# Modulation weights in eighths through a ring of four, six tiles of them on TensorE

## The chip, the cores and the metric

One core of one Trainium2 chip runs the whole program. The metric is the device time of one execution in microseconds (us). Engines are named as in the profile: PE is TensorE (matmuls), PEld its weight loads, DVE VectorE, ACT ScalarE, SP SyncE, which issues the DMAs. PEclk is the granted TensorE clock; 1.00 is 2.4 GHz and half of it is 1.2 GHz.

## The reference

One layer of a transformer is run for 128 context tokens and 512 latent tokens with the same weights: a feed-forward network (FFN0), a token mixer (an mLSTM and an attention branch), and a second feed-forward network. Each of the three is shifted, scaled and gated by a modulation vector that is a product of the conditioning vector with one large matrix, `w_mod`:

```python
def trunk_layer(x, mod, n_pre, n_post, f_in, f_out, mix_w, ctx):
    sh0, sc0, g0, sh1, sc1, g1, sh2, sc2, g2 = jnp.split(mod, N_MOD, axis=-1)
    h = rms_norm(x, n_pre[0]) * (1 + sc0) + sh0
    x = x + 0.5 * g0 * rms_norm(swiglu(h, f_in[0], f_out[0]), n_post[0])
    h = rms_norm(x, n_pre[1]) * (1 + sc1) + sh1
    y, st = token_mixer(h, *mix_w, ctx)
    x = x + g1 * rms_norm(y, n_post[1])
    ...
# reference():
        mod_ctx = (jax.nn.silu(c_ctx) @ w_mod[l] + b_mod[l])[None, None, :]
        mod_lat = (jax.nn.silu(c) @ w_mod[l] + b_mod[l])[:, None, :]
```

Here D_MODEL is 1024, D_FF 2816, N_MOD 9: `w_mod` has 1024 rows and 9216 columns, and only two vectors, one of each group of tokens, are multiplied with it.

## The kernel before

Matrices are streamed from HBM in tiles of 512 KB (128 partitions x 1024 numbers) through four `raw` buffers. Every fp32 weight is split into a high and a low part: ACT casts the high part (`whi`, L1441), DVE subtracts it for the low one (`wlo`, L1979), and PE makes three products (high-high, low-high, high-low). SP issues the loads in program order from one queue; the semaphores on which it waits are those by which a buffer comes free. All orders are written out by hand, engine by engine.

FFN0 runs in three phases p=0, 1, 2 over its 2816 inner columns. A phase has input products (in p=0 as eight-wide loops at L819 to L821, in p=1 and p=2 partly as pairs of seven products i=0..6 at L789 to L791) and then output work: in p=0 and p=1 eight out tiles v=0..7 (`out_tile`, L926 to L928), in p=2 the *border*. An out tile with v other than 3 and 7 has two halves o=0, 1 of 15 matmuls each. The splits of tile v+2 are made on ACT and DVE while PE works at tile v; the cast must wait until PE has left the tile whose buffer it takes. The border adds up FFN0's last out tiles by rows of 128 tokens (`row_w`, L891 to L893), updates the residual `x_tok`, normalises it (L2267 is the first step of that on DVE), and at once starts the mixer's first product with `first_w` (L1012 to L1014).

The first columns of `w_mod` are done at the start; 14 later tiles of 512 columns (n=0..13), each with eight blocks of 128 rows (k=0..7), are worked off inside FFN0 beside the products. Two ways are in use:

- *Multiplied:* DVE multiplies every block by the vectors' numbers and adds it into `macc` (`over_k`: `ts` at k=0, L2343, else `stt`, L2346; two of them for a block, one for each group of tokens). When all eight k are in, PE sums over the partitions with 0/1 weights `pick` (`sum_mod`, L973): four matmuls, one for each quarter of the 128 columns of the array. The trace records each of these fp32 matmuls twice.
- *Direct:* PE multiplies the block as it was loaded with the vectors as weights (`silc_win`) (`direct_mod`, L987). The block's k decides the quarter: even k goes to quarters 0 and 1, odd k to quarters 2 and 3, half of the 512 columns each.

Before, a transfer (`load_mod`, L524) brings two k (512 KB, a quarter of a tile), the ring `mw` has two such places, tiles 7 to 10 are direct and the other ten multiplied. A direct call has two k, so four matmuls, in all four quarters; the 16 calls stand in the pairs n=0..7 of p=1 after the products i=1 and i=4. `sum_mod` stands in out tiles v=2 and v=5 and in two of the pair loops. DVE multiplies some blocks beside the pairs of p=1.

Of the kernel before, what the change touches and what calls it, by code (L numbers as in the profile page):

```python
# [21 lines left out]
P = 128  # L22
# [30 lines left out]
MOD_PARTS, MOD_RING = 4, 2  # L53
PART_K = KC // MOD_PARTS
FIRST_K = KC - PART_K
MOD_DIRECT = (7, 8, 9, 10)
PAIR_PARTS = tuple(((n, part), (n, part + 1)) for n in MOD_DIRECT for part in (0, 2))
MOD_ORDER = ([(n, part) for n in range(MOD_DIRECT[0]) for part in range(MOD_PARTS)]
             + [one for pair in PAIR_PARTS for one in pair]
             + [(n, part) for n in range(MOD_DIRECT[-1] + 1, MOD_LATER) for part in range(MOD_PARTS)])  # L60
# [86 lines left out]
def build(nc, a):  # L147
    ctx = ExitStack()
    with ctx:
# [57 lines left out]
        mw = at("mw", [P, MOD_RING * PART_K, MOD_W], F32, mw_at)  # L207
        macc_at = mw_at + MOD_RING * PART_K * MOD_W * 4
# [26 lines left out]
        def row_home(l, u):  # L235
            one, two = blocks[l], others[l]
            if l == 0:
                return ((mw_at, mw_at + whole), (mw_at + 2 * whole, two), (one, one + whole), (one + 2 * whole, one + 3 * whole),
                        (one + 4 * whole, two + 4 * whole), (two + whole, two + 2 * whole))[u]
            if l == 2:  # L240
                at_ = (one, two)[u % 2] + u // 2 * 2 * whole
                return at_, at_ + whole
            return ((one, one + whole), (one + 2 * whole, one + 3 * whole), (one + 4 * whole, two + 4 * whole),
                    (two, two + whole), (two + 2 * whole, two + 3 * whole))[u]
# [4 lines left out]
                   for u, home in enumerate(((others[0] + 3 * whole, mw_at + 3 * whole),  # L249
                                             (mw_at + 4 * whole, cst_at + 5 * P * 4)))]  # L250
# [257 lines left out]
        def _(sp):  # L508
# [4 lines left out]
            def load_mod(n, part):  # L513
                where = MOD_ORDER.index((n, part))
                if where >= MOD_RING:
# [3 lines left out]
                    else:  # L519
                        sp.wait_ge(mod_mul, 2 * PART_K * parts_until(before, False))  # L520
                slot = where % MOD_RING
                src = a["w_mod"][n][:, part * PART_K * MOD_W:(part + 1) * PART_K * MOD_W]
                to = mw[:, slot * PART_K:(slot + 1) * PART_K, :].rearrange("p k c -> p (k c)")
                sp.dma_start(to, src).then_inc(mod_in[slot], 16)  # L524
# [38 lines left out]
            def ffn(f, base):  # L563
                j0 = 0
                for p, nj in enumerate(PHASES):
# [18 lines left out]
                    if f == 0 and p == 0:  # L584
                        load_mod(0, 0)
                        load_mod(0, 1)
                        for u in range(4, 8):
                            load_in(u)
                            if u > 5:
                                load_mod(0, u - 4)  # L590
                        for u in range(8, tiles):
                            load_in(u)
                            load_mod(u // 4 - 1, u % 4)
                        for v in range(4):
                            load_out(v)
                            load_mod(3, v)
                        for v in range(4, KC):
                            load_out(v)
                            if v < 6:
                                load_mod(4, 2 * v - 8)  # L600
                                load_mod(4, 2 * v - 7)
                            elif v == 7:
                                load_mod(5, 0)
                                load_mod(5, 1)
                    elif f == 0 and p == 1:
                        load_in(0)
                        load_mod(5, 2)
                        load_mod(5, 3)
                        load_in(1)
                        load_in(2)  # L610
                        load_mod(6, 0)
                        load_mod(6, 1)
                        load_in(3)
                        load_mod(6, 2)
                        load_mod(6, 3)
                        for n in SEVEN[1]:
                            for one in PAIR_PARTS[n]:
                                load_mod(*one)
                            load_next(2 * n + 4)
                            load_next(2 * n + 5)  # L620
                        load_mod(11, 0)
                        load_mod(11, 1)
                        load_out(4)
                        load_out(5)
                        load_mod(11, 2)
                        load_mod(11, 3)
                        load_out(6)
                        load_mod(12, 0)
                        load_out(7)
                        load_mod(12, 1)  # L630
                    elif f == 0 and p == 2:
                        for u in range(4):
                            load_in(u)
                            if u < 2:
                                load_mod(12, 2 + u)
                            elif u == 2:
                                load_mod(13, 0)
                                load_mod(13, 1)
                            else:
                                load_mod(13, 2)  # L640
                                load_mod(13, 3)
# [54 lines left out]
            load_post(0)  # L696
            load_residual(a["x_tok"], slice(2, NT))
            mix(2, RAWS)
# [63 lines left out]
        def _(pe):  # L762
            mm, tp = pe.matmul, pe.transpose

            def seven(f, p, n, base):
                g = SEVEN_FROM[f][p] + n
                gt, ut = pair_tiles(base, n)
                for i in range(7):
# [24 lines left out]
                    if f == 0 and p == 1 and i in (1, 4):  # L793
                        direct_mod(*PAIR_PARTS[n][i // 4])
                    if f == 0 and i == 2:
                        if p == 1 and n == 0:
                            sum_mod(6)
                        elif p == 2 and n == 0:
                            sum_mod(13)
# [2232 lines left out]
```

## Time and profile before

| what | us |
|---|---|
| median of 3 runs (1717.27 to 1719.05) | 1718.79 |
| the profiled execution, its own time | 1718.85 |
| its span in the trace | 1716.9 |
| PE busy | 1684.5 (98%) |
| PEld busy | 1545.1 (90%) |
| DVE busy | 1104.6 (64%) |
| ACT busy | 733.3 (43%) |
| chain that ended last: PE / DVE / ACT / DMA | 87% / 5% / 4% / 2% |

FFN0 with everything that the change touches lies in the first 532 us of the span: p=0 until some 213 us, p=1 until some 387, p=2 with the border until 532. A row of the timeline gives the start, the duration, the engine and line, the operation, and in brackets how long the engine sat idle before it and what ended that. Rows of PE overlap, since a matmul's duration contains its way through the array: the distance of two starts says what one costs. "x8" joins eight like records in a row.

### The profile page before, as it was taken

How to read it: one execution, taken by the hardware profiler on the slowest of the kernel's cores; microseconds unless marked ns; L12 is line 12 of the kernel's file. 1: busy time of each engine (PE TensorE's matmuls, PEld its weight loads, DVE VectorE, ACT ScalarE, POOL GpSimd, SP SyncE). 2: the span in 40 equal slices, each digit the busy share in tenths (PEclk: the TensorE clock that was granted, in tenths of full speed). 3: DMA queues.
4: the chain of work that ended last, by engine and by line, in shares of the span. 5: the costliest groups of instructions: out<-in, count | busy, mean ns of one | idle time of the engine just before them, and what ended most of it. 6: DMA issues, size and time to landing. Idle time of an engine off the chain costs nothing.

```text
span 1716.9 us, 27871 instructions
## 1 busy us (share of the span) xinstructions
PE 1684.5 (98%) x11255; PEld 1545.1 (90%) x11255; DVE 1104.6 (64%) x1881; ACT 733.3 (43%) x1370; POOL 0.2 (0%) x4
## 2 busy tenths in 40 slices
PE   8999999999999999999999999999999999999998
PEld 6899799879979989999999988989989988998997
DVE  5688787769855424555536877775546844882785
ACT  6332244314565322343355555553474433541453
POOL 0000000000000000000000000000000000000000
PEclk9999999999999999999999999999999999999999
DMA  9344544542424225332342311102522221322234
GB/s 376 121 147 152 163 169 147 180 140 75 139 95 148 74 74 108 91 100 80 82 155 80 114 53 42 41 23 68 208 73 76 81 92 62 96 89 86 73 96 151
DMA packets 60966, 189.65 MB, mean 110 GB/s; under 512 B 7928, under 2 KB 17064, under 8 KB 58920
## 3 DMA queue, kind: packets, MB, share of 16 engines
q1 hardware_dynamic: 60840, 187.89, 33.6%
q8 instruction: 89, 1.46, 0.3%
q14 instruction: 37, 0.30, 0.1%
HBM read 170.67 MB, written 16.54 MB: 109 GB/s over the span
## 4 chain that ended last, share of the span: by engine, by line
PE 87%; DVE 5%; ACT 4%; DMA 2%; issue 1%; DVEq 0%; ACTq 0%
PE psum L819 9%; PE psum L821 9%; PE psum L820 9%; PE psum L789 8%; PE psum L790 7%; PE psum L791 7%; PE psum L926 4%; PE psum L927 3%; PE psum L928 3%; PE psum L1347 2%; PE psum L1329 2%; PE psum L891 2%; PE psum L893 2%; PE psum L892 2%; PE psum L1307 2%
## 5 line engine op out<-in xcount | busy, mean ns | idle before, releaser
L1979 DVE TENSOR_TENSOR wlo<-raw,whi 128x1024 fp32r<-128x1024 f32 x120 | 146.9, 1224 | 278.0 <-ACT whi L1441 277.8
L1441 ACT CAST whi<-raw 128x1024 fp32r<-128x1024 f32 x120 | 125.6, 1047 | 248.9 <-PE psum L928 131.4
L819 PE MATMUL psum<-g_hi,whi 128*128 128x320 f32 x656 | 209.5, 319 | 0.2 <-ACT gate L1797 0.2
L821 PE MATMUL psum<-g_hi,wlo 128*128 128x320 f32 x656 | 202.8, 309 | 0.0
L820 PE MATMUL psum<-g_lo,whi 128*128 128x320 f32 x656 | 202.8, 309 | 0.0
L819 PEld LDWEIGHTS psum<-g_hi,whi 128*128 128x128 f32 x656 | 123.2, 188 | 4.9 <-issue 1.9
L926 PE MATMUL psum<-whi,g_hi 128*128 128x512 f32 x320 | 126.4, 395 | 0.0
L927 PE MATMUL psum<-wlo,g_hi 128*128 128x512 f32 x320 | 125.8, 393 | 0.0
L928 PE MATMUL psum<-whi,g_lo 128*128 128x512 f32 x320 | 125.4, 392 | 0.0
L820 PEld LDWEIGHTS psum<-g_lo,whi 128*128 128x128 f32 x656 | 123.3, 188 | 0.7
L821 PEld LDWEIGHTS psum<-g_hi,wlo 128*128 128x128 f32 x656 | 123.2, 188 | 0.0
L2346 DVE SCALAR_TENSOR_TENSOR macc<-mw,silc,macc 128x512 f32<-128x512 f32 x140 | 95.5, 747 | 3.5 <-DMA mw<-in_w_mod 3.1
L819 PE MATMUL psum<-h_hi,whi 128*128 128x320 f32 x272 | 84.6, 311 | 2.3 <-DVE sb L2462 2.3
L821 PE MATMUL psum<-h_hi,wlo 128*128 128x320 f32 x272 | 84.1, 309 | 0.0
L820 PE MATMUL psum<-h_lo,whi 128*128 128x320 f32 x272 | 84.1, 309 | 0.0
L926 PEld LDWEIGHTS psum<-whi,g_hi 128*128 128x128 f32 x320 | 60.7, 190 | 15.0 <-issue 2.5
L928 PEld LDWEIGHTS psum<-whi,g_lo 128*128 128x128 f32 x320 | 60.8, 190 | 12.8
L927 PEld LDWEIGHTS psum<-wlo,g_hi 128*128 128x128 f32 x320 | 60.8, 190 | 12.4
L789 PE MATMUL psum<-h_hi,whi 128*128 128x320 f32 x220 | 69.0, 314 | 2.9 <-DVE y L2497 2.5
L789 PE MATMUL psum<-t_hi,wlo 128*128 128x320 f32 x228 | 71.0, 311 | 0.0
L789 PE MATMUL psum<-t_hi,whi 128*128 128x320 f32 x228 | 70.5, 309 | 0.0
L791 PE MATMUL psum<-t_hi,whi 128*128 128x320 f32 x228 | 70.5, 309 | 0.0
(449 smaller groups left out, 4473.6 us busy)
## 6 DMA issues: line engine op xcount, KB each, us to landing
raw<-in_w_ffn_in SPq DMA_DIRECT2D x88, 512.0 KB, 3.7
raw<-in_w_mix SPq DMA_DIRECT2D x77, 512.0 KB, 4.1
mw<-in_w_mod SPq DMA_DIRECT2D x56, 512.0 KB, 4.5
raw<-in_w_ffn_out SPq DMA_DIRECT2D x44, 512.0 KB, 3.6
mw<-in_w_mod SPq DMA_DIRECT2D x8, 1024.0 KB, 16.1
gate<-gate_keep SPq DMA_DIRECT2D x24, 320.0 KB, 4.7
gate_keep<-gate SPq DMA_DIRECT2D x20, 320.0 KB, 4.7
x_keep<-x_tok SPq DMA_DIRECT2D x2, 2560.0 KB, 9.0
```

The source lines that it names most:

```text
L789: mm(out, wh[:, k, :], th[:, k, :], start=(first and k == 0), stop=False, skip_group_check=more)
L790: mm(out, wh[:, k, :], tl[:, k, :], start=False, stop=False, skip_group_check=more)
L791: last = mm(out, wl[:, k, :], th[:, k, :], start=False, stop=(k == KH - 1), skip_group_check=more)
L819: mm(out, wh[:, k, :], hi[:, k, cols], start=(k == 0), stop=False)
L820: mm(out, wh[:, k, :], lo[:, k, cols], start=False, stop=False)
L821: last = mm(out, wl[:, k, :], hi[:, k, cols], start=False, stop=(k == nk - 1))
L926: mm(out, g_hi[:, j, tok], wh[:, o, :], start=(j == 0), stop=False)
L927: mm(out, g_hi[:, j, tok], wl[:, o, :], start=False, stop=False)
L928: return mm(out, g_lo[:, j, tok], wh[:, o, :], start=False, stop=(j == KC - 1))
L1441: copy((to or whi[t.slot])[:, :, :], raw[t.raw][:, :, :]).then_inc(w_hi, 1)
L1979: tt(lo[:, :, :], raw[t.raw][:, :, :], hi[:, :, :].bitcast(F32), ALU.subtract).then_inc(raw_free, 1)
L2346: last = stt(acc, w, by, acc, ALU.mult, ALU.add)
```

## The change

The diff's core; helper lines that only follow are cut.

```diff
-MOD_PARTS, MOD_RING = 4, 2
-FIRST_K = KC - PART_K
-MOD_DIRECT = (7, 8, 9, 10)
+MOD_RING, FIRST_K = 4, 5
+MOD_DIRECT = (6, 7, 8, 9, 10, 11)
+SLOT_OUT = ([(4, 0), (4, 1), (4, 2), (7, 0)], [(4, 3), (4, 4), (4, 5), (7, 1)], [(7, 2)], [(4, 6), (4, 7), (7, 3)],
+            [(5, 0), (7, 4)], [(5, 1), (5, 2), (7, 5)], [(5, 3), (5, 4), (7, 6)], [(5, 5), (5, 6), (5, 7), (7, 7)])
+SLOT_PAIR = [[((6, 8, 9, 10)[n // 2], 4 * (n % 2) + o) for o in range(4)] for n in range(8)]
+SLOT_OUT2 = ([(12, 0), (11, 0)], [(12, 1), (12, 2), (12, 3), (11, 1)], [(12, 4), (12, 5), (12, 6), (11, 2)], [(12, 7), (11, 3)],
+             [(13, 0), (11, 4)], [(13, 1), (13, 2), (13, 3), (11, 5)], [(13, 4), (13, 5), (13, 6), (11, 6)], [(13, 7), (11, 7)])
...
             mix(L_GATE, 2)
             load_post(0)
+            mix(2, RAWS)
             load_residual(a["x_tok"], slice(2, NT))
-            mix(2, RAWS)
...
-                    if f == 0 and p == 1 and i in (1, 4):
-                        direct_mod(*PAIR_PARTS[n][i // 4])
+                    if f == 0 and p == 1 and i in (1, 2, 3, 5):
+                        direct_mod(*SLOT_PAIR[n][{1: 0, 2: 1, 3: 2, 5: 3}[i]])
+                    if f == 0 and i == 2 and n == 0:
+                        sum_mod(5 if p == 1 else 13)
...
+                        if f == 0 and o == 0:
+                            direct_mod(*(SLOT_OUT2 if p else SLOT_OUT)[v][-1])
...
-            def direct_mod(n, part):
+            def direct_mod(n, k):
...
-                for o in range(PART_K):
-                    k = part * PART_K + o
-                    for half in range(2):
-                        last = mm(mod_part(2 * (k % 2) + half, half), silc_win[:, k, skip:skip + MOD_COLS],
-                                  mw[:, slot * PART_K + o, half * MOD_HALF:(half + 1) * MOD_HALF], start=False, stop=False)
+                for half in range(2):
+                    last = mm(mod_part(2 * (k % 2) + half, half), silc_win[:, k, skip:skip + MOD_COLS],
+                              mw[:, slot, half * MOD_HALF:(half + 1) * MOD_HALF], start=False, stop=False)
...
-                            if f == 0 and v in (2, 5):
-                                mod = (4, 11)[p] + v // 5
+                            if f == 0 and v == 4:
+                                mod = (4, 12)[p]
...
+                        if f == 0:
+                            split(Tile(base + 2 * n + 5), row_weights(0, 3, base + 2 * n + 2)[0], gt.n + 3)
+                            split(Tile(base + 2 * n + 6), row_weights(0, 4, base + 2 * n + 2)[0], ut.n + 3)
...
-                for u in range((3, 5, 3)[l], ROW_TILES[l]):
+                for u in range((5, 5, 3)[l], ROW_TILES[l]):
...
+                            if f == 0 and v not in (0, 4):
+                                multiply_slot((SLOT_OUT2 if p else SLOT_OUT)[v])
+                            elif f == 0 and p == 0 and v == 0:
+                                multiply_slot(SLOT_OUT[0])
...
+                            if f == 0 and (v == 4 or p == 1 and v == 0):
+                                multiply_slot((SLOT_OUT2 if p else SLOT_OUT)[v])
```

In words:

- **Transfers.** One k a transfer (256 KB), a ring of four places; 112 transfers instead of 56. In the first stage of p=0, five instead of six k of tile 0 are taken after the normalised rows.
- **Direct tiles.** Tiles 6 to 11 are direct, 0 to 5, 12 and 13 are multiplied. A direct call has one k, so two matmuls, in two of the four quarters. There are 48 calls: one in every out tile of p=0 (tile 7) and of p=1 (tile 11), behind o=0 or, at v=3 and 7, behind the tile, and four in every pair of p=1 (behind i=1, 2, 3 and 5).
- **Multiplied blocks.** None beside the pairs of p=1; tiles 4, 5, 12 and 13 beside the out tiles, before the split in most tiles, behind it (`multiply_slot` at the loop's end) at v=4 of both phases and v=0 of p=1. `sum_mod` stands at v=4 and in the pair n=0.
- **Border.** Row weights u=3 and 4 are split in the last pair of p=2; at the border only u=5 is left, and some buffers change places. SP issues two tiles of the mixer's weights before the 1.5 MB of residual rows instead of behind them.

SP at the first out tiles of p=1, before (`raw` from `w_ffn_out` are out tiles, those from `w_ffn_in` belong to p=2; "x2" joins two like ones):

```order
L511 DMA raw_69<-in_w_ffn_out 128x1024 [waits raw_free]
L511 DMA raw_70<-in_w_ffn_out 128x1024 [waits raw_free]
L524 DMA mw<-in_w_mod 128x1024 [waits mod_mul] x2
L511 DMA raw_71<-in_w_ffn_out 128x1024 [waits raw_free]
L524 DMA mw<-in_w_mod 128x1024 [waits mod_mul]
L511 DMA raw_72<-in_w_ffn_out 128x1024 [waits raw_free]
L524 DMA mw<-in_w_mod 128x1024 [waits mod_mul]
```

And now; `mod_mul` counts DVE's multiplications, `mod_pe` direct calls:

```order
L512 DMA raw_69<-in_w_ffn_out 128x1024 [waits raw_free]
L512 DMA raw_70<-in_w_ffn_out 128x1024 [waits raw_free]
L524 DMA mw<-in_w_mod 128x512 [waits mod_mul]
L524 DMA mw<-in_w_mod 128x512 [waits mod_pe]
L512 DMA raw_71<-in_w_ffn_out 128x1024 [waits raw_free]
L524 DMA mw<-in_w_mod 128x512 [waits mod_mul] x3
L524 DMA mw<-in_w_mod 128x512 [waits mod_pe]
L512 DMA raw_72<-in_w_ffn_out 128x1024 [waits raw_free]
```

The first `mod_mul` row brings (12, 3) and waits for the product with (12, 0); (11, 1), which PE takes in out tile v=1, is the `mod_pe` row behind it.

DVE at out tiles v=0 and 1 of p=1, before (the first of a tile's products, with `pick`, stands ahead of v=0's split):

```order
L1979 TENSOR_TENSOR wlo_76<-raw_70,whi_74 128x1024 [waits w_hi]
L2026 TENSOR_TENSOR g_lo<-sb_80,g_hi 128x640 [waits g_hi_s]
L2352 COPY pick<-pick_row 128x32 [waits rows_zero,mod_done,ev0,ev1]
L2352 COPY pick<-pick_row 128x32
L2343 TENSOR_SCALAR macc<-mw,silc 128x512 [waits mod_in0]
L2343 TENSOR_SCALAR macc<-mw,silc 128x512
L2346 SCALAR_TENSOR_TENSOR macc<-mw,silc,macc 128x512 [waits mod_mul] x2
L2346 SCALAR_TENSOR_TENSOR macc<-mw,silc,macc 128x512 [waits mod_mul,mod_in1]
L2346 SCALAR_TENSOR_TENSOR macc<-mw,silc,macc 128x512 [waits mod_mul] x3
L1979 TENSOR_TENSOR wlo_75<-raw_71,whi_73 128x1024 [waits w_hi]
```

And now:

```order
L1969 TENSOR_TENSOR wlo_76<-raw_70,whi_74 128x1024 [waits w_hi]
L2016 TENSOR_TENSOR g_lo<-sb_80,g_hi 128x640 [waits g_hi_s]
L1969 TENSOR_TENSOR wlo_75<-raw_71,whi_73 128x1024 [waits w_hi,ev0,ev1]
L2342 COPY pick<-pick_row 128x32 [waits mod_done,rows_zero]
L2342 COPY pick<-pick_row 128x32
L2333 TENSOR_SCALAR macc<-mw,silc 128x512 [waits mod_in0]
L2333 TENSOR_SCALAR macc<-mw,silc 128x512
L2336 SCALAR_TENSOR_TENSOR macc<-mw,silc,macc 128x512 [waits mod_mul,mod_in2]
```

The split of tile v+2 (`wlo_75<-raw_71`) has moved ahead of the products with (12, 0).

PE in the pairs of p=1, before, around the first direct call:

```order
L791 MATMUL psum<-t_hi_1_170,wlo_75 128x320
L987 MATMUL psum<-mw,silc_win 32x256 [waits mod_in0,cols_in]
L987 MATMUL psum<-mw,silc_win 32x256 x3
L789 MATMUL psum<-h_hi,whi_74 128x320 [waits ld_x4_then_act_kept,ld_x3_then_prod_lo]
L790 MATMUL psum<-h_lo,whi_74 128x320
```

And now, around one of the 48:

```order
L779 MATMUL psum<-t_hi_1_170,whi_73 128x320
L974 MATMUL psum<-mw,silc_win 32x256 [waits mod_in0]
L974 MATMUL psum<-mw,silc_win 32x256
L777 MATMUL psum<-h_hi,wlo_75 128x320 [waits ld_x4_then_act_kept,ld_x3_then_prod_lo]
L778 MATMUL psum<-h_lo,wlo_75 128x320
```

A call has two matmuls instead of four, and there are three times as many calls.

## Rows read from the trace of the kernel before

**Rows 1.** The page, busy time of the engines.

```profile
PE 1684.5 (98%) x11255; PEld 1545.1 (90%) x11255; DVE 1104.6 (64%) x1881; ACT 733.3 (43%) x1370; POOL 0.2 (0%) x4
```

**Rows 2.** Waits of PE by line: releaser, us in total, times, longest.

```profile
PE psum L973 <- DVE macc L2346: 4.1, 2, 2.2
PE psum L789 <- DVE y L2497: 2.5, 1, 2.5
PE psum L891 <- DVE row_w L1979: 2.3, 1, 2.3
PE psum L863 <- DVE y L2267: 2.3, 1, 2.3
PE psum L819 <- DVE sb L2462: 2.3, 1, 2.3
PE psum L1012 <- DVE g_lo L2272: 1.0, 1, 1.0
```

**Rows 3.** Busy time by windows: window, length, then each engine; PEclk third last.

```profile
213.00:320.00 107.00, 107.00 (x776) 97.29 (x775) 82.60 (x138) 48.89 (x93) 0.00 (x0) 1.00 0.46 154
362.00:371.00 9.00, 6.80 (x29) 4.60 (x28) 3.88 (x5) 0.00 (x0) 0.00 (x0) 0.81 0.40 121
384.00:393.00 9.00, 6.42 (x43) 5.65 (x46) 8.86 (x15) 3.49 (x7) 0.00 (x0) 1.00 0.01 3
```

**Rows 4.** Timeline of PE around a direct call in a pair of p=1.

```profile
216.42 0.31 PE L790 MATMUL psum<-t_lo,wlo 128*128 128x320 f32 x1
216.57 0.31 PE L791 MATMUL psum<-t_hi,wlo 128*128 128x320 f32 x1
216.81 0.64 PE L987 MATMUL psum<-mw,silc_win 128*32 128x256 f32 x8
217.38 0.41 PE L789 MATMUL psum<-h_hi,whi 128*128 128x320 f32 x1
217.63 0.30 PE L790 MATMUL psum<-h_lo,whi 128*128 128x320 f32 x1
```

**Rows 5.** Timeline of PE in the mixer: matmuls in two halves of the array.

```profile
985.51 1.31 PE L1347 MATMUL psum<-sbb,av 128*64 128x128 f32 x20
986.76 1.13 PE L1307 MATMUL psum<-ak,aq 64*128 64x256 f32 x8
```

**Rows 6.** Timeline of PE, first and last matmul of half a tile (p=1, v=5).

```profile
359.50 0.39 PE L926 MATMUL psum<-whi,g_hi 128*128 128x512 f32 x1
...
362.68 0.39 PE L928 MATMUL psum<-whi,g_lo 128*128 128x512 f32 x1
```

**Rows 7.** Timeline of ACT, then DVE, in out tiles v=5 and 6 of p=1.

```profile
359.76 1.05 ACT L1441 CAST whi<-raw 128x1024 fp32r<-128x1024 f32 x1 [5.75 <-PE psum L928]
371.17 1.05 ACT L1441 CAST whi<-raw 128x1024 fp32r<-128x1024 f32 x1 [10.37 <-PE psum L928]
373.57 0.88 DVE L2343 TENSOR_SCALAR macc<-mw,silc 128x512 f32<-128x512 f32 x2
```

**Rows 8.** DMA issues: count, KB, median us to landing; then one of the chain.

```profile
cs<-in_state_C SPq DMA_DIRECT2D x2, 256.0 KB, 2.9
o_x<-x_tok SPq DMA_DIRECT2D x2, 256.0 KB, 2.0
akc<-in_cache_k SPq DMA_DIRECT2D x1, 256.0 KB, 2.8
358.54 3.90 DMA mw<-in_w_mod
```

**Rows 9.** Timeline of DVE ahead of two waits of PE (58.8 and 386.8).

```profile
55.22 2.73 DVE L2346 SCALAR_TENSOR_TENSOR macc<-mw,silc,macc 128x512 f32<-128x512 f32 x4
...
379.77 2.74 DVE L2346 SCALAR_TENSOR_TENSOR macc<-mw,silc,macc 128x512 f32<-128x512 f32 x4 [1.34 <-DMA mw<-in_w_mod]
```

**Rows 10.** Timeline at the border: ACT, then DVE.

```profile
483.44 1.05 ACT L1441 CAST first_w<-raw 128x1024 fp32r<-128x1024 f32 x1 [3.66 <-DMA raw<-in_w_mix]
...
487.35 0.75 DVE L2267 TENSOR_SCALAR y<-x_tok,roots 128x1024 f32<-128x1024 f32 x1 [0.38 <-ACT roots L1550]
```

More of the change, by code:

```diff
@@ L52 @@
 MOD_HALF = MOD_W // 2
-MOD_PARTS, MOD_RING = 4, 2
-PART_K = KC // MOD_PARTS
-FIRST_K = KC - PART_K
-MOD_DIRECT = (7, 8, 9, 10)
[L57 to L60, printed above, removed]
+MOD_RING, FIRST_K = 4, 5
[5 more added lines that the diff above has]
+             [(13, 0), (11, 4)], [(13, 1), (13, 2), (13, 3), (11, 5)], [(13, 4), (13, 5), (13, 6), (11, 6)], [(13, 7), (11, 7)])
+MOD_ORDER = ([(n, k) for n in range(4) for k in range(KC)]
+             + [one for slots in (SLOT_OUT, SLOT_PAIR, SLOT_OUT2) for slot in slots for one in slot])
 MOD_MULTIPLIED = [n for n in range(MOD_LATER) if n not in MOD_DIRECT]
@@ L237, in row_home @@
             if l == 0:
[L238 to L239 removed]
+                return ((mw_at, mw_at + whole), (mw_at + 2 * whole, two), (one, one + whole), (two + whole, cst_at + 5 * P * 4),
+                        (one + 4 * whole, two + 4 * whole), (one + 2 * whole, one + 3 * whole))[u]
             if l == 2:
@@ L511, in load, with load_mod @@
                 sp.dma_start(raw[t.raw][:, :, :].rearrange("p k c -> p (k c)"), src).then_inc(raw_in[t.raw], 16)
-            def load_mod(n, part):
-                where = MOD_ORDER.index((n, part))
+            def load_mod(n, k):
+                where = MOD_ORDER.index((n, k))
                 if where >= MOD_RING:
@@ L519, in load_mod, with load_slot @@
                     else:
-                        sp.wait_ge(mod_mul, 2 * PART_K * parts_until(before, False))
+                        sp.wait_ge(mod_mul, 2 * parts_until(before, False))
                 slot = where % MOD_RING
-                src = a["w_mod"][n][:, part * PART_K * MOD_W:(part + 1) * PART_K * MOD_W]
-                to = mw[:, slot * PART_K:(slot + 1) * PART_K, :].rearrange("p k c -> p (k c)")
-                sp.dma_start(to, src).then_inc(mod_in[slot], 16)
+                src = a["w_mod"][n][:, k * MOD_W:(k + 1) * MOD_W]
+                sp.dma_start(mw[:, slot, :], src).then_inc(mod_in[slot], 16)
+            def load_slot(slot):
+                for n, k in slot:
+                    load_mod(n, k)
             def pick(tiles, n):
@@ L594, in ffn @@
-                        for v in range(4):
+                            load_mod(u // 4 - 1, u % 4 * 2)
+                            load_mod(u // 4 - 1, u % 4 * 2 + 1)
+                        for v in range(KC):
                             load_out(v)
[L596 to L604, printed above, removed]
-                    elif f == 0 and p == 1:
[L606 to L615, printed above, removed]
-                        for n in SEVEN[1]:
[L617 to L622, printed above, removed]
@@ L2064, in seven @@
                     if p == 2:
-                        for u in range(1, 3):
+                        for u in range(1, 3 if f else 4):
                             split(Tile(base + 2 * n + 2 + u), row_weights(2 * f, u, base + 2 * n + 2))
                     pair_product(n, s)
+                    if p == 2 and f == 0:
+                        split(Tile(base + 2 * n + 6), row_weights(0, 4, base + 2 * n + 2))
                     if p < 2:
@@ L2206, in first_normed @@
                     if k >= FIRST_K:
[L2207 removed]
+                        over_k(0, k - FIRST_K)
             def add_square(l, m):
@@ L2275, in first_split @@
                     split(Tile(nxt + u), first_weights(l, u, nxt))
-                for u in range((3, 5, 3)[l], ROW_TILES[l]):
+                for u in range((5, 5, 3)[l], ROW_TILES[l]):
                     split(Tile(base + u), row_weights(l, u, base))
@@ L2352, in pick_rows, with multiply @@
                     copy(pick[:, g * MOD_COLS:(g + 1) * MOD_COLS], pick_row[:, first:first + MOD_COLS])
-            def multiply(n, part, ks=range(PART_K)):
-                if part == 0 and ks.start == 0:
+            def multiply(n, k):
+                if k == 0:
                     dve.wait_ge(rows_zero, 1)
@@ L2358, in multiply, with multiply_slot, later_k @@
                     pick_rows(n)
-                over_k(n, part, ks)
-            def later_k(part):
-                if part == MOD_PARTS - 1:
+                over_k(n, k)
+            def multiply_slot(slot):
+                for n, k in slot[:-1]:
+                    multiply(n, k)
+            def later_k(first, last):
+                if last == KC:
                     dve.wait_ge(pick_in, 2)
                     pick_rows(0)
-                over_k(0, part, range(PART_K))
+                for k in range(first, last):
+                    over_k(0, k)
             def take_rows():
```

117 lines of the change are left out of this document (50 added, 67 removed).

## The prediction

> **What bounds the kernel now.** I read the busy times first. PE is busy 1684.5 of 1716.9 us [rows 1], so the span can shrink only by PE's own work, by PE's waits, or by the start and the end. Next the windows: over the pairs of p=1 PE is busy 107.00 of 107.00 us [rows 3]. Whatever is put between two matmuls there lengthens the span one to one, and work taken from DVE (64% busy) gives nothing by itself. Then PE's waits by line [rows 2]: in the part that the change touches there are seven of 1 us and more, 14.5 us in sum (4.1 + 2.5 + 2.3 + 2.3 + 2.3 + 1.0), and these alone can be won. A wait can cost more than its length: around the wait at 365 the granted clock is 0.81 over 9 us, around that at 386.8 it is 1.00 [rows 3]. A mean of 0.81 with levels 1 and 0.5 means 9 x 0.19 / 0.5 = 3.4 us at 1.2 GHz, in which 1.7 us of work are lost. Of the six waits over 1.9 us, four (the two at L973, L891, L863) are followed by it and two (L819, L789) are not.
>
> **The change part by part.**
>
> *Direct calls, +22.0.* What one costs I take from the distance of starts: from the last matmul ahead of it (216.57) to the second behind it (217.63) are 1.06 us; two steps of the 320-wide matmuls would be 2 x 0.147 (from 216.42 to 216.57 is one), so the call costs 0.77 [rows 4]. I read its eight records (four matmuls) as two rounds of four, each quarter doing its own matmul's two records one after the other. The new call has two matmuls in two quarters: half the work, but each quarter still has two records to do. The nearest row is one in which the array is split in two: 20 records of L1347 take 985.51 to 986.76, 1.25 us, so ten rounds of two at 0.125 [rows 5]; different parts of the array run beside each other, records of one part do not. A round of 256 columns is then 0.22 to 0.25, two of them 0.43 to 0.50, and some 0.33 of the 0.77 (0.27 to 0.34) are going into and out of the split form. So the new call keeps both rounds and both transitions: 0.77, with half the array idle. Bounds: half of it (0.38), if a call costs by its matmuls, and 0.77; I take 0.77, the end that rows 5 speak for. Calls: 16 are removed and 48 added, 32 x 0.766 = +24.5. Two `sum_mod` fewer (10 become 8; eight records in the same form) give -1.5. In three places a direct call stands right behind a `sum_mod`, so one pair of transitions is shared: 3 x 0.33 = -1.0. Together +22.0; with 0.38 a call it would be 48 x 0.38 - 12.3 - 2.5 = +3.5.
>
> The Trainium skill ("TensorEngine Tiling (Array Packing)", section Tiling Modes, Key Properties) says that a change of the tiling mode drains the engine and that tiles work independently, in parallel. That speaks against cutting calls in half, and the trace agrees: some 0.3 of the 0.77 are no rounds. By that rule, too, the sum would be 1741.
>
> *DVE's multiplications, 0 by themselves.* Two tiles fewer are 32 operations of 0.75, 24 us of an engine that PE seldom waits for. One k more in the first stage falls into gaps of 1.3 us that DVE has there between the steps of the normalisation; if it did not fit, it would cost 0.9.
>
> *New waits, +10.0, and the clock behind them, +5.1.* A direct call makes PE wait for a DMA where before only DVE did. SP issues in order, and a place of the ring of four comes free by the block four earlier. At p=1, (11, 1) stands behind (12, 3), which waits for DVE's product with (12, 0); (11, 5) likewise behind (13, 3) and (13, 0); at p=0, (7, 5) takes the place of (5, 0) itself. All three products now stand behind the split of tile v+2 on DVE, and that split behind ACT's cast, which starts when PE has left the tile before. The chain from the start s of a tile, in rows of v=5 and v=6: the cast starts at s + 0.26 (359.50 to 359.76 [rows 6, 7]); from the cast (371.17) to the first product (373.57) are 2.40, and the two products take 0.88 [rows 7]. So the place is free at s + 3.55, and SP issues at s + 3.6, for (11, 1) and (11, 5) one issue (0.4) later. No row has a load of 256 KB of `w_mod`; others of 256 KB land in 2.0 to 2.9 [rows 8], a lone one of 512 KB in 3.90 [rows 8]. I take 2.8 (a load from HBM of the same size), bounds 2.0 and 3.9. The weights are there at s + 6.4 for (7, 5) and s + 6.8 for the others. PE asks for them behind o=0, 15 matmuls after s: 359.50 to 362.68 are 14 steps, so s + 3.4 [rows 6]. PE waits 3.0 + 3.5 + 3.5 = 10.0 (with 2.0 a load 7.6, with 3.9 13.3). All three lie in tiles of lines 926 to 928, where both waits of before were followed by the low clock; 3 x 1.7 = 5.1, or nothing if the clock holds as at 386.8. (7, 1) is the next closest and lands about when it is asked for; I put it at 0.
>
> The Trainium skill ("DMA: Bandwidth & Descriptors", section Anatomy of one DMA) gives 2.0 us and the bytes by 436 GB/s, an estimate of 2.6 for 256 KB. The rows with 2.8 and 2.9 agree. The three waits would each be 0.2 shorter, and the time 1740.
>
> *Old waits that go, -12.3.* The two waits of `sum_mod` for DVE (4.1 us [rows 2]) go, as tiles 4 and 12 are summed at v=4, after the blocks have long been multiplied: -1.9 - 2.2, and 1.7 of clock each, -7.5. The wait of L819 for L2462 (2.3) stands behind four multiplications, 55.22 to 57.95 [rows 9], which now come before the split: -2.3. The wait of L789 for L2497 (2.5) comes from DVE running late after a wait of 1.34 for a load and the multiplications at 379.77 [rows 9], which are gone from there: -2.5.
>
> *Border, -2.5.* Three waits stand here: L891 2.3, L863 2.3, L1012 1.0 [rows 2]. Splitting u=3 and 4 sooner moves the first one to u=5, whose raw weights land hardly sooner: about 0. The 1.5 MB of residual are issued ahead of the mixer's weights, which keep ACT idle for 3.66 until 483.44 [rows 10]; issued ahead of it they come about 4 us sooner, ACT and DVE split `first_w` sooner, and the normalisation at 487.35 [rows 10] starts some 2.5 earlier. Behind it stands the chain of ACT and DVE for each 128 tokens, which the end of the border follows (the wait at L1012 is its sign), so the 2.5 come through once. Bounds: 0, if the residual (two of its rows are now later by two issues) takes the place of the weights; 9.0, if all three waits and both clock losses go (2.3 + 2.3 + 1.0 + 2 x 1.7). I take 2.5, nearest to the idle time of ACT.
>
> *SP.* It issues 112 instead of 56 transfers at some 0.4; its queue waits for semaphores most of the time, so the 24 us are hidden, save the 0.4 counted above.
>
> Sum, from the profiled execution's 1718.85 (0.06 above the median, so they can be used alike): 1718.85 + 22.0 + 10.0 + 5.1 - 12.3 - 2.5 = **1741**.
>
> **The rivals.**
>
> *A, the loads come in time.* If DVE's split and products were ahead of PE (the cast earlier, loads at 2.0), PE would not wait: 1741 - 15 = 1726. For: DVE has 24 us less to do. Against: the order on DVE, and a cast bound to the end of PE's tile.
>
> *B, old waits stay.* The two waits of `sum_mod` might come back at v=4, if the loads of tiles 4 and 12 are held up by the same queue: 1741 + 7.5 = 1749. For: the ring holds 1 MB before and after, so SP runs no further ahead. Against: in p=0 the blocks of tile 4 are spread over v=0, 1 and 3 and DVE has slack at v=2.
>
> *C, the other side: calls cost by their matmuls.* If the records of two quarters fill one round, as four records of the same form seem to do in [rows 4], and the transitions hide behind the weight loads, a call costs near 0.2 and not 0.77: 48 x 0.2 - 12.3 - 2.5 = -5.2, and if the new waits are hidden as well, 1718.85 - 5.2 - 12.3 - 2.5 = 1699; with the new waits 1714. With the waits, it decides below a price of (14.8 of the removed calls and sums + 12.3 + 2.5 - 15.1) / 48 = 0.30 a call. Against: [rows 5], and the 0.3 outside the rounds. A call of one round (0.77 - 0.22) gives 1741 - 48 x 0.22 = 1730, still slower.
>
> *D, the whole border is won:* 1741 - 6.5 = 1734.5, still slower.
>
> **How the numbers follow.** Forecast (with D and the dearer or cheaper loads in it) 0.74, its own range 1733 to 1749; A, or a call of one round, 0.14, 1725 to 1732; B 0.07; C 0.05, of which 0.02 fall within 0.2%. 0.2% (3.4 us) is about what a measurement of this kernel can tell from no change. From 1725 to 1750 the cases of the forecast, A and B count 0.95 by their centres; their tails and C leave out under 2 in 10. Slower 0.95, same 0.02, faster 0.03.
>
> **What would show it.** The calls: 48 groups of four records at the `direct_mod` line, with 0.77 between the neighbours' normal steps; 0.55 or less fails the largest term. The waits: PE waiting for a DMA `mw` at that line three times, at v=5 of p=0 and at v=1 and 5 of p=1, 3 to 3.5 us each, with PEclk near 0.8 behind them. The old waits: no wait of `sum_mod` for `macc`, none of L819 and L789 in FFN0. The border: ACT's `first_w` some 4 us sooner after the end of p=2, and the first mixer matmul behind the border 2.5 sooner. The forecast is wrong if PE's busy time does not grow by some 20 us, or if a wait that I do not list is longer than 3 us.

## The result and the profile after

The changed kernel takes 1741.84 us (median of 4 runs, 1740.57 to 1743.75), the kernel before on the same chip 1718.92. The ratio is 1.0136, with a 95% interval of 1.0118 to 1.0153: 22.9 us slower. The forecast was 1741.0, from 1725 to 1750. The profiled execution of the changed kernel took 1743.75, with a span of 1741.8; it is 1.9 above the median, and the terms below are read from it.

The page, busy time of the engines, answering to [rows 1]:

```profile
PE 1707.4 (98%) x11303; PEld 1547.4 (89%) x11303; DVE 1084.9 (62%) x1845; ACT 733.3 (42%) x1370; POOL 0.2 (0%) x4
```

DVE has given up 19.7 us of work and PE has taken 22.9 us more. Now the waits of PE by line (releaser, us in total, times, longest), answering to [rows 2]; only those of FFN0 and the border are shown. L974 is `direct_mod`, L876 the border's row product, L848 the normalisation, L999 the mixer's first product:

```profile
PE psum L974 <- DMA mw<-in_w_mod: 12.5, 4, 4.6
...
PE psum L876 <- DVE row_w L1969: 2.0, 1, 2.0
PE psum L999 <- DVE g_lo L2264: 2.0, 2, 1.2
...
PE psum L848 <- DVE y L2259: 0.6, 1, 0.6
```

The waits of `sum_mod` for `macc` (4.1), of L789 (2.5) and of L819 (2.3) are gone, as forecast. In their place stands one line that waits for a DMA, 12.5 us in four waits. Where they are, and what the clock does behind three of them: first PE's timeline (idle time before and what ended it in brackets), then the busy times by windows, PEclk third last.

```profile
161.99 0.63 PE L974 MATMUL psum<-mw,silc_win 128*32 128x256 f32 x4 [0.53 <-DMA mw<-in_w_mod]
...
195.89 1.07 PE L974 MATMUL psum<-mw,silc_win 128*32 128x256 f32 x4 [3.02 <-DMA mw<-in_w_mod]
...
355.05 1.07 PE L974 MATMUL psum<-mw,silc_win 128*32 128x256 f32 x4 [4.35 <-DMA mw<-in_w_mod]
...
392.70 1.07 PE L974 MATMUL psum<-mw,silc_win 128*32 128x256 f32 x4 [4.64 <-DMA mw<-in_w_mod]
```

```profile
195.00:204.00 9.00, 8.11 (x30) 6.01 (x31) 3.03 (x4) 1.05 (x1) 0.00 (x0) 0.81 0.41 152
354.00:363.00 9.00, 7.95 (x27) 5.84 (x28) 1.66 (x3) 1.05 (x1) 0.00 (x0) 0.68 0.48 179
392.00:401.00 9.00, 8.30 (x29) 6.08 (x30) 1.14 (x2) 1.05 (x1) 0.00 (x0) 0.71 0.40 141
```

The four are v=1 and v=5 of p=0 and v=1 and v=5 of p=1: (7,1), (7,5), (11,1) and (11,5). Around the three long ones the mean clock is 0.81, 0.68 and 0.71. The last two of these windows begin before the wait ends, and the clock is low there already while PE stands still, so not all of that is lost work. Cut at the ends of the two waits, they read:

```profile
354.00:355.05 1.05, 0.00 (x1) 0.00 (x1) 1.05 (x2) 0.00 (x0) 0.00 (x0) 0.50 0.76 275
355.05:364.05 9.00, 9.00 (x32) 6.69 (x33) 1.66 (x3) 1.05 (x1) 0.00 (x0) 0.74 0.39 147
392.00:392.70 0.70, 0.00 (x0) 0.00 (x0) 0.36 (x1) 0.00 (x0) 0.00 (x0) 0.50 0.95 366
392.70:401.70 9.00, 9.00 (x32) 6.66 (x33) 1.47 (x2) 1.05 (x1) 0.00 (x0) 0.75 0.33 113
```

So 3.4, 4.7 and 4.5 us at half clock lie behind the waits, in which 1.7 + 2.3 + 2.3 = 6.3 us of work are lost. Two of the expectations below put 7.2 there, which counts the parts inside the waits too.

A direct call in a pair, on PE's timeline, answering to [rows 4]:

```profile
229.73 0.31 PE L779 MATMUL psum<-h_hi,wlo 128*128 128x320 f32 x1
229.97 0.62 PE L974 MATMUL psum<-mw,silc_win 128*32 128x256 f32 x4
230.52 0.41 PE L777 MATMUL psum<-t_hi,whi 128*128 128x320 f32 x1
230.77 0.30 PE L778 MATMUL psum<-t_lo,whi 128*128 128x320 f32 x1
```

Four records, half of those before, and from 229.73 to 230.77 are 1.04 us; less two steps of 0.147 the call costs 0.75. With four matmuls it cost 0.77. The 42 calls that stand alone at the full clock read like this, less their waits (median 0.75 in the pairs, 0.76 in the out tiles). Of the other six, three share a place with a `sum_mod`, and the three behind the long waits run at half the clock.

### The profile page after: what moved, and what is told of

Its sections match the earlier page's. It is cut to its first block, busy times and chain, and to the rows that moved or that the text cites. A ratio compares the mean times of both kernels' runs of the same rounds, so it can differ in the third digit from the quotient of the medians.

```text
span 1741.8 us, 28010 instructions
## 1 busy us (share of the span) xinstructions
PE 1707.4 (98%) x11303; PEld 1547.4 (89%) x11303; DVE 1084.9 (62%) x1845; ACT 733.3 (42%) x1370; POOL 0.2 (0%) x4
## 4 chain that ended last, share of the span: by engine, by line
PE 63%; DVE 3%; ACT 3%; DMA 2%; issue 1%; DVEq 0%; SPq 0%; ACTq 0%
PE psum L804 7%; PE psum L806 6%; PE psum L805 6%; PE psum L777 4%; PE psum L778 4%; PE psum L779 4%; PE psum L1334 2%; PE psum L912 2%; PE psum L913 2%; PE psum L911 2%; PE psum L1316 2%; PE psum L1294 2%; PE psum L876 1%; PE psum L877 1%; PE psum L878 1%; PE psum L1219 1%
## 5 line engine op out<-in xcount | busy, mean ns | idle before, releaser
L804 PE MATMUL psum<-h_hi,whi 128*128 128x320 f32 x272 | 84.5, 311 | 0.0
L2336 DVE SCALAR_TENSOR_TENSOR macc<-mw,silc,macc 128x512 f32<-128x512 f32 x112 | 76.7, 745 | 1.2 <-DMA mw<-in_w_mod 1.2
L777 PE MATMUL psum<-t_hi,wlo 128*128 128x320 f32 x228 | 71.7, 314 | 0.0
L779 PE MATMUL psum<-t_hi,wlo 128*128 128x320 f32 x228 | 70.4, 309 | 0.0
```

The lines of the kernel that those rows point to most:

```text
L777: mm(out, wh[:, k, :], th[:, k, :], start=(first and k == 0), stop=False, skip_group_check=more)
L779: last = mm(out, wl[:, k, :], th[:, k, :], start=False, stop=(k == KH - 1), skip_group_check=more)
L804: mm(out, wh[:, k, :], hi[:, k, cols], start=(k == 0), stop=False)
L2336: last = stt(acc, mw[:, slot, :], by, acc, ALU.mult, ALU.add)
```

## The experiments

Each kernel was timed beside the kernel before on the same chip; the medians of before in these comparisons lie between 1719.2 and 1719.9. Ratios are to before, with 95% intervals. The changed kernel itself was timed beside a before of 1718.92, so a difference between two of these kernels is uncertain by about 1 us.

**What a call costs, on the kernel before.** The 16 direct calls are cut in two each, and nothing else is touched: the same tiles, the same transfers, the same ring.

```diff
-                    if f == 0 and p == 1 and i in (1, 4):
-                        direct_mod(*PAIR_PARTS[n][i // 4])
+                    if f == 0 and p == 1 and i in (1, 2, 4, 5):
+                        direct_mod(*PAIR_PARTS[n][i // 4], (i - 1) % 3)
```

> The kernel before, with each of its 16 direct calls of four matmuls cut in two calls of two (two quarters of the array each), behind products i=1, 2, 4 and 5; transfers, ring and tiles unchanged. Theory (a call costs by its transitions and its two rounds, 0.75 whether it has two or four matmuls): 16 x 0.75 = +12 us, 1731, and PE waits as before. Rival (a call costs by its matmuls): no change, 1719. Rival in between (a call of two matmuls has one round, 0.55): +5.3, 1724.

Measured: 1730.77, ratio 1.0071 (1.0054 to 1.0088). PE does the same matmuls and is 11 us slower. The waits do not stay quite the same in the profiled execution (one for `mw` of 1.1 us is new, and the first wait of `sum_mod` has no low clock behind it), so the price is better read from the rows. PE's timeline around two of the half calls (L986):

```profile
222.57 0.31 PE L791 MATMUL psum<-h_hi,whi 128*128 128x320 f32 x1
222.81 0.62 PE L986 MATMUL psum<-mw,silc_win 128*32 128x256 f32 x4
223.37 0.41 PE L789 MATMUL psum<-h_hi,wlo 128*128 128x320 f32 x1
223.62 0.30 PE L790 MATMUL psum<-h_lo,wlo 128*128 128x320 f32 x1
```

1.05 from 222.57 to 223.62, so 0.76 for half the work of a call that cost 0.77. The price belongs to the place, not to the matmuls; the rival by matmuls (1719) and the one of a single round (1724) fall.

**The same on the changed kernel.** The four calls of a pair are put together in twos, even k and odd k.

```diff
-                    if f == 0 and p == 1 and i in (1, 2, 3, 5):
-                        direct_mod(*SLOT_PAIR[n][{1: 0, 2: 1, 3: 2, 5: 3}[i]])
+                    if f == 0 and p == 1 and i in (1, 4):
+                        for one in SLOT_PAIR[n][i // 4 * 2:i // 4 * 2 + 2]:
+                            direct_mod(*one)
```

> The changed kernel, with the four calls in each pair of p=1 put together in twos (even k and odd k right behind one another, behind i=1 and i=4). Theory of the price by call: 16 places fewer, 16 x 0.75 = -12 us, 1730; a doubled call of four matmuls costs 0.75 to 0.85. Rival by matmuls: no change, 1742. The waits for weights in the out tiles (12.5 us in four) stay in both.

Measured: 1730.52, ratio 1.0063 (1.0047 to 1.0080). Sixteen places fewer give 11.3 us; about 1.0 of it are shorter waits in the profiled execution, where the four are still there (11.5 us instead of 12.5, at the `direct_mod` line, L975):

```profile
PE psum L975 <- DMA mw<-in_w_mod: 11.5, 4, 4.3
```

**Why the loads are late: DVE's products.** The changed kernel, with every product of the out tiles ahead of the split.

```diff
-                            if f == 0 and v not in (0, 4):
-                                multiply_slot((SLOT_OUT2 if p else SLOT_OUT)[v])
-                            elif f == 0 and p == 0 and v == 0:
-                                multiply_slot(SLOT_OUT[0])
+                            if f == 0:
+                                multiply_slot((SLOT_OUT2 if p else SLOT_OUT)[v])
...
-                            if f == 0 and (v == 4 or p == 1 and v == 0):
-                                multiply_slot((SLOT_OUT2 if p else SLOT_OUT)[v])
```

> The changed kernel, with DVE's products at v=4 of both phases and at v=0 of p=1 put ahead of the split again, as in the other tiles. Theory (those products free the ring's places late): the waits of 3.0, 4.35 and 4.64 us for (7,5), (11,1) and (11,5) go, and with them the stretches of halved clock behind them (granted clock 0.81, 0.68 and 0.71 over 9 us: 3.4, 5.8 and 5.2 us at half, 7.2 us of work lost): 1742 - 12 - 7.2 = 1723. Rival (the queue or the landing itself is what is late): the waits stay, 1742, or the split of tile v+2 comes late and PE waits for whi and wlo instead, 1735 and more. If the low clock is not bound to the waits: 1730.

Measured: 1723.74, ratio 1.0027 (1.0015 to 1.0040), 18.1 us below the changed kernel. The three long waits are gone and only that of (7,1) is left; so is the low clock, as the windows of this kernel at the same three places show:

```profile
PE psum L974 <- DMA mw<-in_w_mod: 0.5, 1, 0.5
```

```profile
191.00:200.00 9.00, 9.00 (x42) 6.80 (x40) 6.69 (x9) 1.67 (x2) 0.00 (x0) 1.00 0.44 147
345.00:354.00 9.00, 9.00 (x44) 6.28 (x42) 6.61 (x10) 1.05 (x1) 0.00 (x0) 1.00 0.65 184
385.00:394.00 9.00, 9.00 (x40) 7.43 (x40) 8.02 (x14) 1.14 (x2) 0.00 (x0) 1.00 0.29 103
```

**Or the ring's places?** This kernel leaves DVE's products behind the split and changes only which place of the ring the late blocks take: they are loaded two places sooner. (`multiply_slot` and the direct calls then pick their blocks by tile number instead of by position.)

```diff
-            [(5, 0), (7, 4)], [(5, 1), (5, 2), (7, 5)], [(5, 3), (5, 4), (7, 6)], [(5, 5), (5, 6), (5, 7), (7, 7)])
+            [(5, 0), (7, 4)], [(5, 1), (7, 5), (5, 2)], [(5, 3), (5, 4), (7, 6)], [(5, 5), (5, 6), (5, 7), (7, 7)])
...
-SLOT_OUT2 = ([(12, 0), (11, 0)], [(12, 1), (12, 2), (12, 3), (11, 1)], ...
-             [(13, 0), (11, 4)], [(13, 1), (13, 2), (13, 3), (11, 5)], ...
+SLOT_OUT2 = ([(12, 0), (11, 0)], [(12, 1), (11, 1), (12, 2), (12, 3)], ...
+             [(13, 0), (11, 4)], [(13, 1), (11, 5), (13, 2), (13, 3)], ...
```

> The changed kernel with DVE's products where they are, but the ring in another order: the blocks (7,5), (11,1) and (11,5) are loaded two places sooner, so that each takes a place that PE or DVE has left a tile earlier and none is queued on SP behind a wait for the products of the same tile. Theory (PE waits because the place in the ring comes free late): the three waits (12.0 us) and the low clock behind them (7.2) go, as in the run with the products first: 1742 - 18 = 1724. Rival (the products or the split behind which they stand are themselves on PE's path): PE waits on, for DVE, and the time stays at 1735 to 1742.

Measured: 1727.01, ratio 1.0043 (1.0027 to 1.0058): 14.8 of the 18 us, 3 short of what I expected. PE's waits at its `direct_mod` line (L979), and one of them on the timeline:

```profile
PE psum L979 <- DMA mw<-in_w_mod: 3.1, 3, 1.5
```

```profile
355.24 0.63 PE L979 MATMUL psum<-mw,silc_win 128*32 128x256 f32 x4 [1.46 <-DMA mw<-in_w_mod]
```

The blocks (7,5), (11,1) and (11,5) come in time, with the products as late as before; so it was the ring's place and the queue, and the late products only through them. What is left moved one tile on: now (12,2) and (12,3) come late to DVE, and (11,2) and (11,6), queued behind them, make PE wait 1.46 and 1.16. With waits this short the clock stays at 1.00. The rival (the products are on PE's path themselves) falls.

**Both edits together.** Calls in twos and products first.

> Both edits: the pairs' calls in twos and the products ahead of the split. If the two theories hold and add up: 1742 - 12 - 19 = 1711, below the kernel before by 8 us (0.45%). If either falls, as much less: 1723 to 1730.

Measured: 1713.60, ratio 0.9963 (0.9949 to 0.9977). The two parts add up, to 2.6 us; as far as the profiled executions show, the rest is the border's first wait, which was 2.6 here, with the low clock behind it, and 1.6 without it in the kernel with the products alone. This version is faster than the kernel before.

**The border, on the kernel before.** First the whole border part of the change, then the later residual alone; the second is the first without its other hunks.

```diff
             mix(L_GATE, 2)
             load_post(0)
+            mix(2, RAWS)
             load_residual(a["x_tok"], slice(2, NT))
-            mix(2, RAWS)
```

> The kernel before with the border part of the change alone: row weights u=3 and 4 split in the last pair of p=2, the buffers that this moves, and the residual rows fetched behind two tiles of the mixer's weights. Theory of the prediction: -2.5 us, 1717, from the wait at L863 (2.3 us before, 0.6 in the changed kernel); the first wait of the border (L891, 2.3) stays near 2. Rival: nothing (1719.5), the gain seen at the border of the changed kernel comes from the lighter DVE ahead of it. Other end: all three waits and the low clock behind them go, -9.

> The kernel before with the residual rows 2 to 4 fetched behind two tiles of the mixer's weights, and nothing else. Theory of the prediction (this edit is what moves the normalisation, the sooner split is worth about 0): -2.5 us, 1717, the same as with the whole border part. Rival (the sooner split is what counts): 0, 1719.5, and the wait at L863 stays at 2.3.

Measured: 1716.04 with the whole part, ratio 0.9982 (0.9973 to 0.9991); 1714.91 with the residual alone, ratio 0.9975 (0.9965 to 0.9986). The two lines of the residual do all of it, 3 to 4 us; that the row weights are split sooner adds nothing. The waits at the border and ACT's first `first_w` in the kernel with the residual alone, answering to [rows 2, 10]:

```profile
PE psum L891 <- DVE row_w L1979: 2.3, 1, 2.3
...
PE psum L1012 <- DVE g_lo L2272: 2.0, 2, 1.2
...
PE psum L863 <- DVE y L2267: 0.5, 1, 0.5
```

```profile
480.31 1.05 ACT L1441 CAST first_w<-raw 128x1024 fp32r<-128x1024 f32 x1 [0.77 <-DMA raw<-in_w_mix]
```

The cast starts at 480.31 instead of 483.44, the wait at L863 falls from 2.3 to 0.5, and 1.0 of it comes back at L1012, which waits 2.0 in two places instead of 1.0 in one. The waits alone would make that 0.8 us. What carries the gain is the chain of ACT and DVE that the border's end follows: the normalisation, at 487.35 before [rows 10], and PE's first mixer product behind the border, before and here:

```profile
484.39 0.74 DVE L2267 TENSOR_SCALAR y<-x_tok,roots 128x1024 f32<-128x1024 f32 x1
```

```profile
531.99 0.41 PE L1012 MATMUL psum<-g_hi,whi 128*128 128x320 f32 x1 [1.02 <-DVE g_lo L2272]
529.03 0.41 PE L1012 MATMUL psum<-g_hi,whi 128*128 128x320 f32 x1 [1.23 <-DVE g_lo L2272]
```

Both come 2.96 us sooner.

**Fewer places still.** In the out tiles the changed kernel makes one call per tile. Here, on the kernel with both edits, two k stand at every second tile (v=0, 2, 4, 6), with the blocks spread anew; the lines of p=1:

```diff
+SLOT_OUT2 = ([(12, 0), (11, 0), (11, 1)], [(12, 1), (12, 2), (12, 3)], [(12, 4), (12, 5), (11, 2), (11, 3)], [(12, 6), (12, 7)],
+             [(11, 4), (11, 5), (13, 0)], [(13, 1), (13, 2), (13, 3)], [(11, 6), (11, 7), (13, 4), (13, 5)], [(13, 6), (13, 7)])
```

> The changed kernel with the products first and the pairs' calls in twos, and in the out tiles two k at every second tile (v=0, 2, 4, 6) instead of one k in each; the blocks are spread over the tiles and the ring anew to fit. Eight places fewer in PE's program: 8 x 0.755 = -6 us against 1713.6, so 1707.5, if no load comes late. Rival (by matmuls): 1713.6. Rival (the new spread makes DVE or a load late): a wait of 3 to 5 us in one of the tiles, 1711 to 1716.

Measured: 1705.52, ratio 0.9929 (0.9914 to 0.9945), 8.1 below the kernel with both edits. By the price of a call, 6 are the eight places; for the two or so above that the profiled executions show the wait for (7,1) (0.4), gone with the new order, and the low clock at the border (1.7), which this one lacks. PE waits nowhere for `mw`.

**One place in a pair.** The same, and all four k of a pair behind i=2.

```diff
-                    if f == 0 and p == 1 and i in (1, 4):
-                        for one in SLOT_PAIR[n][i // 4 * 2:i // 4 * 2 + 2]:
-                            direct_mod(*one)
+                    if f == 0 and p == 1 and i == 2:
+                        direct_slot(SLOT_PAIR[n])
```

> The same, and in the pairs all four k in one place behind i=2 (eight matmuls, 16 records). Theory (0.33 for the transitions and 0.216 for each round of four records): four rounds, 0.33 + 4 x 0.216 = 1.19 instead of 2 x 0.765, so 8 x 0.34 = -2.7 us against the kernel with two places, 1705. Rival (a price by the place alone): 8 x 0.765 = -6, 1701.5. Rival (the ring empties in one go, and the raw weights queued behind it on SP come late): a wait in the pairs, 1708 and more.

Measured: 1703.23, ratio 0.9912 (0.9897 to 0.9927). The timeline of one place, now 16 records:

```profile
227.51 0.31 PE L779 MATMUL psum<-h_hi,wlo 128*128 128x320 f32 x1
227.75 1.07 PE L977 MATMUL psum<-mw,silc_win 128*32 128x256 f32 x16
228.75 0.41 PE L777 MATMUL psum<-t_hi,whi 128*128 128x320 f32 x1
229.00 0.31 PE L778 MATMUL psum<-t_lo,whi 128*128 128x320 f32 x1
```

1.49 from 227.51 to 229.00, so the place costs 1.20, where 0.33 + 4 x 0.216 = 1.19 was expected. That separates the two parts of the price: each round of four records 0.216, and 0.33 for going in and out. The rival of a price by the place alone (0.77) falls.

A place of the changed kernel settles one point more: whether a call of four records does two rounds of two, or one round and some least price of a place. In the pair n=0 of p=1 a call and a `sum_mod` (L962, eight records) stand in one place:

```profile
222.52 0.31 PE L779 MATMUL psum<-h_hi,whi 128*128 128x320 f32 x1
222.76 0.41 PE L974 MATMUL psum<-mw,silc_win 128*32 128x256 f32 x2
222.77 0.41 PE L962 MATMUL psum<-macc,pick 128*32 128x256 f32 x2
223.00 0.39 PE L974 MATMUL psum<-mw,silc_win 128*32 128x256 f32 x2
223.01 0.80 PE L962 MATMUL psum<-macc,pick 128*32 128x256 f32 x6
223.75 0.42 PE L777 MATMUL psum<-t_hi,wlo 128*128 128x320 f32 x1
224.00 0.31 PE L778 MATMUL psum<-t_lo,wlo 128*128 128x320 f32 x1
```

The call's records start in twos, with two of the sum beside them each time. From 222.52 to 224.00 are 1.48, so the place costs 1.19, which is 0.33 and four rounds, a round being one record in each quarter that has one left; twelve records in full rounds of four would be three, 0.98. Quarters 2 and 3 have records of both to do (the call has k=1), four each, and it is their number that counts.

**The border in the fastest kernel.** The same with row weights u=3 and 4 split at the border again.

> The fastest kernel so far (1703.2; one place in the pairs, four places fewer in each phase's out tiles) with row weights u=3 and 4 split at the border again; the residual stays behind the mixer's weights. Theory (the sooner split is worth about 0, since u=5 holds PE instead): 1703 +- 1.5. Rival (it is worth one of the waits, 1.3 to 2.3 us and 1.7 of clock): 1705 to 1707.

Measured: 1703.86, ratio 0.9912 (0.9898 to 0.9926): no difference that can be told from 1703.23. As on the kernel before, the sooner split buys nothing, so it can be left out.

## Why the prediction was right, term by term

The total is 0.8 from the median, closer than its terms deserve. By the rows:

| term | forecast | measured | from |
|---|---|---|---|
| direct calls and sums | +22.0 | +21.4 | 48 x 0.755 - 16 x 0.765 = +24.0; two sums fewer -1.6; three shared places -1.0 |
| new waits | +10.0 | +12.5 | the four waits at L974 |
| clock behind them | +5.1 | +6.3 | PEclk 0.81, 0.74, 0.75 over 9 us from the ends of the waits |
| old waits | -12.3 | -11.4 | waits gone; PE's lead at L819 grew by 2.0, at L789 by 1.9 |
| border | -2.5 | -2.6 | PE's lag of before, from 387 to 532 us |
| start of the kernel | 0 | -1.4 | the wait for the first constants, 3.5 instead of 4.3, and one behind it |

The measured terms add up to 24.8, and the two spans differ by 24.9. That is closer than it should be: at the end of the border PE lags by 24.1 (the first mixer product at 556.12 instead of 531.99), so up to there the terms are 0.7 too large, and as much comes in behind. The term at the start is one of single executions, it differs as much between profiles of other kernels here. Measured against the median, 1.9 below this execution, the errors of the terms (+2.5) and this offset (-1.9) nearly cancel, and that was luck.

*The calls.* The largest step rested on the reading that a quarter does its own two records one after the other, taken from the row with two halves [rows 5]. The trace of after (0.75 for two matmuls), the cut calls on the kernel before (+11 for 16 places), the place with four k (1.20) and the place shared with a sum (1.19) say the same. Rule and row agreed as well: of 0.75, 0.33 are no rounds, which fits the drain that the Trainium skill ("TensorEngine Tiling (Array Packing)", section Tiling Modes, Key Properties) states for a change of the tiling mode.

*The new waits.* All three stand where they were put, and the chain can be followed for (11,1): the rows of PE, ACT, DVE and SP in the tile that starts at 347.14.

```profile
347.14 0.39 PE L911 MATMUL psum<-whi,g_hi 128*128 128x512 f32 x1
...
347.39 1.05 ACT L1428 CAST whi<-raw 128x1024 fp32r<-128x1024 f32 x1 [5.49 <-PE psum L913]
...
349.89 0.88 DVE L2333 TENSOR_SCALAR macc<-mw,silc 128x512 f32<-128x512 f32 x2
...
350.79 0.81 SPq L524 DMA_DIRECT2D mw<-in_w_mod  x2
```

The cast starts 0.25 after the tile, the products end 3.6 after it, SP issues 3.65 after it, and the load of (11,1), the second of the two, some 0.4 later. Up to here the forecast is met within 0.1. The load then takes until 355.05, some 3.8 us, where I took 2.8. That is the mis-sized term: of three waits, the two of p=1 are 0.85 and 1.1 longer than the 3.5 of the forecast (4.35 and 4.64), that of p=0 is as forecast (3.02). (By the forecast's own terms the 3.5 should read 6.8 - 3.4 = 3.4.) The page of after has the row that was missing, all loads of a k (count, KB, median us to landing):

```profile
mw<-in_w_mod SPq DMA_DIRECT2D x112, 256.0 KB, 3.8
```

Half the bytes take 3.8 where the 512 KB of before took 4.5 (page of before, 56 loads). I had sized it by loads in quieter places [rows 8], and for a load that is alone this holds: in the trace of after, from 45 us on, 13 loads of a k were issued with no other load in flight and took 2.66 to 3.04 (median 2.75); 41 were issued with one other in flight, median 3.7. SP's rows for (7,5), and for (11,5) with the load ahead of it:

```profile
192.85 0.33 SPq L524 DMA_DIRECT2D mw<-in_w_mod  x1
```

```profile
388.05 0.81 SPq L524 DMA_DIRECT2D mw<-in_w_mod  x2
```

The load for (7,5) is alone and takes 3.0. Those for (11,1) and (11,5) are the second of two: the first lands after 3.0 and 2.9, the second after 3.8 and 4.2. The forecast gave the second place only its 0.4 of issue; for these two the bound of 3.9 was the better value. The estimate of 2.6 from the Trainium skill ("DMA: Bandwidth & Descriptors", section Anatomy of one DMA), a fit of the page to DMAs that GpSimd issues, is near the loads that are alone here, which SP issues, and not near those behind another; the measurement decides. (7,1), put at 0, waits 0.53: its load too was issued 0.4 behind another, and took 3.5. Why the second takes longer was not tried.

*The clock.* I gave every new wait the 1.7 us that such a stall had cost in the trace of before. It was more behind the two longer ones (1.7, 2.3, 2.3), and the link to the lines 926 to 928 that I saw there does not hold: see the last section.

*Old waits and border.* Both came as forecast in size, and for the border the runs on the kernel before show the cause that was named: the residual, not the split. `first_w` comes 3.1 us sooner there, where about 4 were put, and the normalisation 3.0, where 2.5 were put. The medians there moved by 3 to 4.

*Rivals.* A (loads in time) is what the kernel with the products first shows, 1723.7, where 1726 was worked out. B and C did not occur; the price of a call is 2.5 times that from which C would have decided. C's price of a call was wrong, but what it put beside it is seen in the last kernels: with fewer places and no new waits, the waits that went leave a gain, and the time is 1703.

## What to carry to other kernels

Small matmuls that split the array in column groups cost by the place where they interrupt the stream and by the records of the fullest group (here 0.33 us for going in and out and 0.216 for each round), not by their number, so collect them until every group has work; the 19.7 us taken from an engine with slack did not pay for 32 more such places. When PE is made to consume a DMA directly, follow the ring's place back to the instruction that frees it, through every engine's queue, and size the load by others that have as many loads ahead of them. And a stall of PE is dearer than its length if the clock falls behind it, so a sum over waits should carry that as a term of its own.

## What the runs showed of the hardware

The low clock behind a wait is not bound to a place in the program. The wait of L819 in the first tiles was 2.3 us in the trace of before and left the clock at 1.00; the same wait of 2.3 us in the kernel with the later residual, of which the program is the same up to there, was followed by 0.81. The windows of before and of that kernel:

```profile
54.00:63.00 9.00, 6.73 (x55) 5.96 (x54) 8.13 (x13) 2.31 (x4) 0.00 (x0) 1.00 0.35 117
54.00:63.00 9.00, 6.74 (x45) 5.96 (x44) 8.21 (x14) 2.26 (x3) 0.00 (x0) 0.81 0.35 117
```

In the first 560 us of all twelve traces here, the wait for the first constants aside, none of PE's 26 waits of 1.0 to 1.7 us had a slower clock behind it (the one of 1.46 above had 1.00). All six of 3.0 to 4.6 us had one, and of the 25 between, from 1.8 to 2.6, 17 had and 8 had not. Around the waits of 4.35 and 4.64 the clock stayed low for longer, and it had fallen before PE went on (0.50 in the windows that end with the wait). What decides in the cases between was not tried.
